# Two chained blocks on one core: GpSimd's low parts in pieces of 256 columns, later places for two sums of squares, first tiles one by one

## What is computed

```python
def second_block(x, c, ...):
    ...
        y = hybrid_mixer(h, w_in[l], ...)              # ends in merged @ w_out
        x = x + (1.0 + gt1) * rms_norm_2(y, post1_w[l])
        h = rms_norm_2(x, pre2_w[l]) * (1.0 + sc2) + sh2
        y = swiglu_ffn(h, ffn_w_in[l], ffn_w_out[l])
        x = x + (1.0 + gt2) * rms_norm_2(y, post2_w[l])
    return x

def swiglu_ffn(h, w_in, w_out):
    gate, up = jnp.split(h @ w_in, 2, axis=-1)
    return (jax.nn.silu(gate) * up) @ w_out
```

## Time and profile before

| | |
|---|---|
| median of 3 runs | 2648.02 us (2646.36 to 2648.84) |
| the profiled execution | 2642.91 us, span 2641.1 us |
| PE busy | 2422.4 us (92%), 11312 matmuls |
| GpSimd (POOL) busy | 1104.2 us (42%) |
| VectorE busy | 1071.2 us (41%) |
| ScalarE busy | 613.0 us (23%) |
| TensorE clock granted | 0.94 of full, mean |
| DMA | 84 GB/s, mean |

### The profile page before, as it was taken

One profiled execution on the slowest core, in us unless ns is written; L12 is line 12 of the kernel. 1 busy time (PEld: TensorE's weight loads), 2 busy tenths in 40 slices (PEclk: granted clock), 3 DMA queues, 4 the chain that ended last, 5 costly groups with the idle time before them and its releaser, 6 DMA issues.

```text
span 2641.1 us, 29887 instructions
## 1 busy us (share of the span) xinstructions
PE 2422.4 (92%) x11312; PEld 1939.4 (73%) x11312; DVE 1071.2 (41%) x1125; ACT 613.0 (23%) x668; POOL 1104.2 (42%) x1036
## 2 busy tenths in 40 slices
PE   4998887988699998999988999989889999999996
PEld 3777776767387876787766777877678888888875
DVE  6774544245521324143036633564673310233406
ACT  4543332132421222112011223222321100111111
POOL 3332222343131322222154413346566667666674
PEclk8999997999798998889788999999899999999998
DMA  3333333010211111101101113434243333333343
GB/s 137 115 108 104 103 103 112 24 56 24 102 45 44 41 48 41 64 24 56 40 26 47 42 50 108 145 126 135 65 143 95 97 102 103 101 98 95 104 152 119
DMA packets 64911, 220.83 MB, mean 84 GB/s; under 512 B 7344, under 2 KB 8512, under 8 KB 64832
## 3 DMA queue, kind: packets, MB, share of 16 engines
q1 hardware_dynamic: 61376, 207.14, 24.6%
q10 hardware_dynamic: 3456, 12.58, 1.2%
HBM read 194.53 MB, written 25.17 MB: 83 GB/s over the span
## 4 chain that ended last, share of the span: by engine, by line
PE 74%; DVE 9%; issue 5%; ACT 4%; DVEq 3%; DMA 2%; POOL 2%; ACTq 1%; POOLq 1%; SPq 0%
PE PG L725 27%; PE PG L522 16%; PE PG L569 13%; PE PG L960 5%; POOL WL L445 1%; PE PX L668 1%; PE PX L925 1%; DMA ADA<-ada_w 1%; PE PG L545 1%; PE PX L664 1%; DVE WK L1592 1%; DVE ADA L1601 1%; PE PX L592 1%; DMA WRAW<-hg_w 1%; PE PX L505 1%
## 5 line engine op out<-in xcount | busy, mean ns | idle before, releaser
L442 POOL TENSOR_TENSOR TOUCH<-TOUCH 128x2 f32<-128x2 f32 x282 | 86.9, 308 | 1441.1 <-PE PG L569 504.4
L445 POOL TENSOR_TENSOR WL<-WRAW,WH 128x1024 fp32r<-128x1024 f32 (+2 forms) x282 | 662.4, 2349 | 42.1 <-issue 3.4
L522 PE MATMUL PG<-UH,WH 128*128 128x512 f32 x832 | 329.6, 396 | 18.6 <-ACT WK L1296 8.0
L522 PE MATMUL PG<-UL,WH 128*128 128x512 f32 x832 | 327.0, 393 | 0.0
L522 PE MATMUL PG<-UH,WL 128*128 128x512 f32 x832 | 326.6, 393 | 0.0
L725 PE MATMUL PG<-UL,WH 128*128 128x512 f32 x800 | 312.6, 391 | 0.0
L443 POOL TENSOR_SCALAR WH<-WRAW 128x1024 fp32r<-128x1024 f32 (+2 forms) x282 | 299.8, 1063 | 0.0
L725 PE MATMUL PG<-UH,WH 128*128 128x512 f32 x688 | 268.5, 390 | 1.4 <-POOL WL L445 1.4
L725 PE MATMUL PG<-UH,WL 128*128 128x512 f32 x688 | 267.7, 389 | 0.0
L569 PE MATMUL PG<-UH,WH 128*128 128x512 f32 x544 | 240.6, 442 | 6.5 <-POOL WL L445 6.5
L569 PE MATMUL PG<-UL,WH 128*128 128x512 f32 x544 | 228.6, 420 | 0.0
(11 more groups left out here) (451 smaller groups left out, 3830.0 us busy)
## 6 DMA issues: line engine op xcount, KB each, us to landing
WRAW<-up_w SPq DMA_DIRECT2D x88, 512.0 KB, 3.5
ADA<-ada_w SPq DMA_DIRECT2D x48, 512.0 KB, 4.5
WRAW<-down_w SPq DMA_DIRECT2D x48, 512.0 KB, 3.6
WRAW<-out_w SPq DMA_DIRECT2D x24, 512.0 KB, 3.6
WRAW<-zg_w SPq DMA_DIRECT2D x24, 512.0 KB, 3.5
gates<-STG ACTq DMA_DIRECT2D x24, 512.0 KB, 2.6
WK<-gates SPq DMA_DIRECT2D x24, 512.0 KB, 3.3
H<-x SPq DMA_DIRECT2D x16, 512.0 KB, 5.6
```

Of the source, the lines that this page charges most:

```text
L442: pool.tensor_tensor(TOUCH[:, 0:2], TOUCH[:, 2:4], TOUCH[:, 4:6], ALU.add)
L445: pool.tensor_tensor(WL[:, r, 0:n], WRAW[:, r, 0:n], WH[:, r, 0:n].bitcast(F32), ALU.subtract).then_inc(w_split, 1)
L522: mm = pe.matmul(PG[:, 2 * s + half, :], w[:, r, P * k:P * k + P], x[:, k, tok], start=first and k == 0 and n == 0, stop=last and k == kbs ...
```

## The change

Four edits. (1) `split_tile` writes WL in pieces of 256 columns, four instructions for 1024, and counts `w_split` on the last. (2) The first two half-width tiles of out2a and up0 are multiplied one after the other (`half_as_made`), each block by block. (3) The `half_sum` of the pre-norm of half 0 comes after the sixth tile of out2b instead of the fifth, that of half 1 after unit 4 of up0 instead of unit 3. (4) On ACT and DVE the steps of hidden unit 4 move ahead of the root, and those of unit 5 between the two groups of four input blocks of half 1.

```diff
+LOW_PIECE = 256
...
-                pool.tensor_tensor(WL[:, r, 0:n], WRAW[:, r, 0:n], WH[:, r, 0:n].bitcast(F32),
-                                   ALU.subtract).then_inc(w_split, 1)
+                for at in range(0, n, LOW_PIECE):
+                    c = slice(at, at + LOW_PIECE)
+                    ins = pool.tensor_tensor(WL[:, r, c], WRAW[:, r, c], WH[:, r, c].bitcast(F32), ALU.subtract)
+                ins.then_inc(w_split, 1)
...
+            def half_as_made(t, bank, hi, ready, count):
+
+                pe.wait_ge(w_split, t + 1)
+                for k in range(KB):
+                    pe.wait_ge(ready, count + k + 1)
+                    for m_, (w, x) in enumerate(((WH, hi), (WH, UL), (WL, hi))):
+                        mm = pe.matmul(PG[:, bank, :], w[:, t % 2, P * k:P * k + P], x[:, k, 0:512],
+                                       start=k == 0 and m_ == 0, stop=k == KB - 1 and m_ == 2)
+                mm.then_inc(tile_done, 1)
+
             pe.wait_ge(slot_free[0], UNIT0["out2a"] // 2)
-            for k in range(KB):
-                pe.wait_ge(sp_lo, 8 + k + 1)
-                for g in range(2):
...
+            for g in range(2):
+                half_as_made(TILE0["out2a"] + g, g, MH, sp_lo, 8)
...
-                    if (u, g) == (2, 0):
+                    if (u, g) == (2, 1):
                         half_sum(2, PRE_ACC, pre_acc, 3)
...
+                    pe.wait_ge(slot_free[0], UNIT0[up] // 2)
+                    for g in range(2):
+                        half_as_made(TILE0[up] + g, g, UH, norm_lo, 32)
+                    for n in range(1, 6):
+                        if n == 1:
+                            half_sum(1, POST_ACC, post_acc, 6)
+                        if n == 5:
+                            half_sum(3, PRE_ACC, pre_acc, 6)
+                        t = TILE0[up] + 2 * n
+                        pe.wait_ge(slot_free[n % 2], n // 2 + UNIT0[up] // 2)
                         for g in range(2):
...
+                            partial(t + g, g, 2 * (n % 2) + g, 8, u_half(0)).then_inc(tile_done, 1)
...
-                with pe.Fori(2 - 2 * hf, 11) as i:
+                with pe.Fori(3 - 3 * hf, 11) as i:
...
             hidden_hi(0, 1, 1)
+            hidden_hi(0, 2, 0)
             half_root2(PRE_RS, 3, 7)
             for j in range(4):
                 u2_high(1, j)
-            hidden_hi(0, 2, 0)
+            hidden_hi(0, 2, 1)
             for j in range(4, 8):
                 u2_high(1, j)
-            hidden_hi(0, 2, 1)
...
             hidden_lo(0, 1, 1, HL2, 0)
+            hidden_lo(0, 2, 0, HL2, 0)
             dve.wait_ge(norm_rs, 8)
             dve.wait_ge(tile_done, TILE0["up0"])
             u2_blocks(1, 0, 4)
-            hidden_lo(0, 2, 0, HL2, 0)
+            hidden_lo(0, 2, 1, HL2, 0)
             u2_blocks(1, 4, 8)
-            hidden_lo(0, 2, 1, HL2, 0)
```

More of the change, by code:

```diff
@@ L970, in half_sum @@
                 pe.matmul(PX[:, bank, :], ONES[:], WK[:, acc, 512:1024], start=False, stop=True).then_inc(norm_ms, 1)
-            pe.wait_ge(slot_free[0], UNIT0["out2a"] // 2)
-            for k in range(KB):
-                pe.wait_ge(sp_lo, 8 + k + 1)
-                for g in range(2):
[L976 to L982, removed]
+            def half_as_made(t, bank, hi, ready, count):
[6 more added lines that the diff above has]
+                mm.then_inc(tile_done, 1)
+            pe.wait_ge(slot_free[0], UNIT0["out2a"] // 2)
+            for g in range(2):
+                half_as_made(TILE0["out2a"] + g, g, MH, sp_lo, 8)
             for u in range(1, 4):
```

## The result

| | before | changed kernel |
|---|---|---|
| median, us | 2648.02 | 2658.14 |
| runs, from to | 2645.89 to 2650.14 (7) | 2653.48 to 2662.44 (7) |
| profiled execution, span | 2642.91, 2641.1 | 2658.14, 2656.4 |
| ratio, 95% interval | | 1.0037 [1.0026, 1.0049] |

Slower by 10 us, beyond the 0.2% bound and inside the range. The profiled execution of the changed kernel is at its median, that of the kernel before 5.1 us under its own, so the two traces differ by 15.3 us where the medians differ by 10.1.

A forecast was written before the change was run, and what follows sets the result against it. PE was taken as the bound (74% of the chain that ended last, DVE 9%), paying where it waits for WL or DVE. Seven terms summed to +4.0 us on the median, so 2652 us, with 2634 to 2664 for eight in ten.

The forecast's parts named there:

- Term 6: Places where PE waits for DVE: DVE is freed sooner by the pieces, -6 us, between -2 and -9.
- term 2: Gate, out1, hg and glu: WL on PE's path gets longer by pieces and DVE turns, +16 us, between 8 and 20.
- term 3: out2a: first tiles one by one remove PE waits, plus 2.7 us of clock; -9.5 us, between -5 and -10.
- 4: out2b to up0: half 0's half_sum no longer waits and unit 1 starts sooner, -4.7 us, between 0 and -7.
- Term 5: up0, half_sum of half 1: -2.5 us, then +2.5 us from DVE turns behind the root; pair between -8 and +8.
- term 1: down0 and down1: 16 tiles each pay 0.45 us for the pieces, +7.2 us, between 0 and 9.
- 7: Last residual: 16 short DVE instructions take turns with the pieces and slow the splits, +1 us.
- pieces do not let DVE in where it hurts: Rival: WLs grow by 0.45 us only, total -8, or -12 if the clock stays up; chance 0.25 shared with another rival.
- only the order counts: Rival: piece cost and turns cancel everywhere but in down, total -10 us; chance 0.25 shared with another rival.
- The splits become bound: Rival: in dense half-width stretches, some 65 us, splits with turns hold up PE by 22 to 24 us, 2662; chance 0.15.

The follow-up runs named there:

- the order alone: Edits 2 to 4 put into the kernel before, WL left whole: 2629.57 us, ratio 0.9929 against the kernel before.
- e2: Only WL in pieces of 256 columns (edit 1) put into the kernel before, its order kept: 2680.00 us, ratio 1.0119.
- h1: Edits 2 to 4, with pieces of 256 columns only in hg_w and out1_w: 2643.16 us, ratio 0.9982 against the kernel before.
- o2: The order alone without the edit at out2a, WL whole: 2638.17 us, ratio 0.9955 against the kernel before.
- f2: Edits 2 to 4, with pieces of 512 in out2a, out2b and up0 and of 256 in rg_w: 2620.85 us, ratio 0.9891 against the kernel before.
- g1: Edits 2 to 4, WL whole except pieces of 128 columns in gate_w: 2647.86 us in a single run.

## Why the prediction was right, and where its sizes were off

Below, the delay of PE at the same matmul (counted from the first) in two traces, and what it grew by in each stretch. Up to out2a and in down the changed kernel is taken against the order alone, whose code is the same there but for the pieces and whose profiled execution is near its median (2628.73 against 2629.57); from out2a to down0 against the kernel before.

| stretch | term | predicted | in the traces |
|---|---|---|---|
| rg_w (to 190 us) | 6 | -2.7 | -3.3 |
| hg heads (to 397) | 2 | +4.2 | +7.6 |
| out1 (to 460) | 2 | +4.2 | +6.9 |
| gate (to 640) | 2 | +6.6 | +9.2 |
| 640 to 850 | 6 | | -6.3 |
| 850 to out2a, with glu | 2, 6 | +1.3, and -3.3 with the row above | +1.4 |
| out2a | 3 | -9.5 | -9.0 |
| out2b to unit 1 of up0 | 4 | -4.7 | -4.6 |
| units 1 to 5 of up0 | 5 | 0 | +0.3 |
| down0 | 1 | +3.6 | +3.6 |
| down1 with the last residual | 1, 7 | +4.6 | +5.4 |
| sum | | +4.0, with term 2 rounded to 16 | +11.2 |

Two rows need the other traces beside them. hg takes 207.4 to 212.3 us in the ten traces with whole WLs there and 210.4 in their mean; the order alone is one of the short ones. The three with pieces of 256 (the changed kernel, e2, h1) take 215.6, 215.1 and 213.6. So the pieces cost some 4.3 us there and not 7.6. And from 640 to 850 the order alone is one of the four long traces; against the others the changed kernel gains some 3 us and not 6.3. The two corrections cancel in the sum.

**Right.** The mechanism, and with it the sign of every term. The waits moved as listed: 9.53 at gate where I said 9, none at the second half_sum, the new ones in up0 and down, and no load or queue of SP in the place of any. Terms 3 and 4 came within half a us. Term 5 did too, but by luck: the delay fell by 4.8 us up to where the old half_sum ended and rose by 5.2 behind it, where I had 2.5 and 2.5. At gate pieces of 256 start 1.66 us apart where alone it is 0.68, so a turn cost GpSimd 1.0 us beside long DVE instructions, where I had 0.94, and a piece cost DVE (1.57 + 1.74)/2 - 1.28 = 0.37, where I had 0.40. The rival "pieces do not let DVE in where it hurts" fell at gate (6.50 us against its 3.7), and "only the order counts" fell with the pieces alone, at +31.5 us. "The splits become bound" is what units 1 to 5 show in part: pieces of 256 turned 6.25 us of gain that the order alone has there into +0.3.

By the rule of the Trainium skill ("SBUF — State Buffer", "Who interferes with whom") a turn would cost GpSimd the whole 1.28 us. As an estimate by it, pieces of 256 and of 128 columns would start 0.68 + 1.28 = 1.96 and 0.42 + 1.28 = 1.70 us apart. The traces have 1.66 and 10.99/8 = 1.37. The rows decide: three quarters.

**The step that was mis-sized is term 2**, 16 us where the traces have some 22, by two omissions. One is the clock behind the longer wait at gate. From the wait for its first tile to its end, in the order alone and then in the changed kernel (columns as in the earlier trace rows):

```profile
551.00:639.94 88.94, 79.81 (x337) 65.13 (x336) 49.29 (x30) 22.12 (x21) 34.54 (x22) 0.94 0.14 42
```

```profile
561.90:660.31 98.41, 82.20 (x338) 66.90 (x337) 43.36 (x30) 22.13 (x21) 49.11 (x46) 0.90 0.13 38
```

The idle time of PE grew by 9.47 - 2.39 = 7.1 us, where I had 6.6. But its busy time over the same matmuls grew as well, by 2.4 us, at a granted clock of 0.90 instead of 0.94. That is a cost that no term held, though term 3 had counted the same thing where a wait goes. It is no chance of one trace: gate takes 88.8 to 89.1 us in the ten traces with whole WLs there, and 98.2 in both with pieces of 256.

In hg one pair of traces would say the same, and would mislead. The order alone, o2 and the changed kernel, over the same matmuls:

```profile
190.09:398.07 207.98, 182.14 (x1086) 148.26 (x1084) 105.50 (x146) 69.82 (x69) 53.57 (x38) 0.96 0.32 109
```

```profile
191.16:402.81 211.65, 185.80 (x1086) 151.12 (x1084) 105.49 (x146) 70.11 (x69) 55.25 (x38) 0.93 0.32 107
```

```profile
186.77:402.33 215.56, 185.70 (x1085) 151.11 (x1084) 100.52 (x148) 69.70 (x69) 57.99 (x74) 0.92 0.32 106
```

The code of o2 up to here is that of the order alone, its WLs are whole, and its busy time is that of the changed kernel. So a cost in clock is not shown in hg, and the 4.2 us that I had there fit the 4.3 of the means.

The other omission is out1, where I charged the split ahead 0.4 us; its WL went from 2.61 to 5.00, since long instructions of DVE met it too. The stage takes 69.0 and 69.3 us in the changed kernel and e2, 66.8 in h1, and 60.2 to 62.3 in the ten traces with whole WLs there. h1 shows that the share of hg and out1 is real time: 13.6 us, nearer to 4.3 + 6.9 = 11.2 than to the 8.4 that I had.

**Term 6 had the right size, and two of its places are shown.** Its part in rg_w is shown by f2 (4.5 to 5.5 us). The other is the wait in ml0 that went from 8.0 to 5.6 us. What the traces have from 640 to 850 us came as clock, for a reason that is open.

**What the prediction missed as a whole** is that it priced the sum and not the alternatives. It wrote that in dense rows "a row of four or more gains only 0.4, and the WL pays three turns more", but never asked which stages have only such rows. That sentence alone says that gate and out1 should keep a whole WL, and term 1 says it of down.

## What to carry to other kernels

Two engines that take turns instruction by instruction, as these two do here, share by count: cutting an instruction into n pieces hands the other engine n turns, so cut only the side that is not on the critical path at that place, and no finer than the waiting engine needs. Decide it per stage, by what PE's wait ends with there. And give parts of a change that do not need each other their own measurement: here a gain of 0.7% was bundled with a loss of 1.2%. Before a few us between two traces are given a cause, look how far traces of the same code lie apart at that place.

## What the runs showed of the hardware

The turns are strict in these traces and do not depend on how short the piece is. A GpSimd piece that takes 0.46 us alone (128 columns, the first gate tile of g1) lets in a full DVE instruction of 1024 columns each time. DVE then runs nearly undisturbed, 1.30 and 1.47 us against 1.28, while GpSimd writes its 1024 columns in 10.99 us instead of 3.2. Also unexpected is how much arrives as granted clock. At gate 2.4 us of busy time came with 7.1 us of idle time. And the same code differs by its clock from trace to trace: in the ten traces with whole WLs in hg PE is busy between 180.0 and 185.8 us over the same matmuls, at 0.96 down to 0.92.
